# A hybrid mLSTM / Hyena / expert-FFN backbone on one core: the ends of its two expert layers rearranged

## What is computed

```python
def moe_ffn(xt, rg_w, rg_b, re_w, re_b, w13, w2):
    g_prob = softmax(xt @ rg_w + rg_b);  g_w, g_idx = top_k(g_prob, 1)
    e_logits = (xt @ re_w + re_b).reshape(T, 4, 8)[group g_idx]
    e_w, e_idx = top_k(softmax(e_logits), 2);  e_w = e_w / sum(e_w)
    ...                                    # rows sorted by expert
    gate, up = split(xblk @ w13[e], 2);  yb = (silu(gate) * up) @ w2[e]
    return segment_sum(yb * row_w, row_tok)

for i in range(2):
    hl = hl + g1 * mixer_i(norm(hl))
    hl = hl + g2 * moe_ffn(norm(hl), ...)
return rmsnorm(hl, final_g)
```

## Time and profile before

| | us |
|---|---|
| median of 3 runs | 2341.99 (2341.27 to 2342.74) |
| profiled execution, own time | 2345.15 |
| its span in the trace | 2343.4 |
| PE busy in it | 2043.4 (87%) |
| mean DMA rate | 253 GB/s |

### The profile page before, as it was taken

One profiled execution on the slowest core, in us unless ns is written; L12 is line 12 of the kernel. 1 busy time (PEld: TensorE's weight loads), 2 busy tenths in 40 slices (PEclk: granted clock), 3 DMA queues, 4 the chain that ended last, 5 costly groups with the idle time before them and its releaser, 6 DMA issues. The chain is left out here.

```text
span 2343.4 us, 20663 instructions
## 1 busy us (share of the span) xinstructions
PE 2043.4 (87%) x7552; PEld 901.8 (38%) x7552; DVE 819.8 (35%) x1601; ACT 363.7 (16%) x770; POOL 238.5 (10%) x523
## 2 busy tenths in 40 slices
PE   5999899999979969988888859999996998888882
PEld 2555344444433434433223224444554443332320
DVE  2777402256353642211111115463734221111113
ACT  2111202212213121111111103110002111111111
POOL 0000000000000002221112210000000221112220
PEclk9999999999989979999999989999996999999996
DMA  9797612320104569999999963221253999999994
GB/s 348 286 377 293 214 45 90 108 87 22 63 3 143 211 231 372 406 407 407 407 406 406 403 255 128 69 90 36 100 223 117 380 406 407 407 407 406 406 403 155
DMA packets 185926, 593.62 MB, mean 253 GB/s; under 512 B 23880, under 2 KB 41536, under 8 KB 178505
## 3 DMA queue, kind: packets, MB, share of 16 engines
q1 hardware_dynamic: 159230, 549.58, 60.5%
q10 hardware_dynamic: 14412, 25.59, 3.1%
q0 software_dynamic: 12160, 16.83, 2.0%
HBM read 572.68 MB, written 42.31 MB: 262 GB/s over the span
## 5 line engine op out<-in xcount | busy, mean ns | idle before, releaser
L537 PE MATMUL bank<-w,xT 128*64 128x512 f32 x1920 | 436.7, 601 | 55.0 <-DMA w<-in_moe_w 46.8
L557 PE MATMUL bank<-w,hT 128*64 128x512 f32 x1168 | 281.9, 626 | 71.6 <-DMA w<-in_moe_w 64.1
L537 PEld LDWEIGHTS bank<-w,xT 128*64 128x64 f32 x1920 | 151.8, 138 | 327.5 <-issue 270.1
L727 DVE COPY hT<-bank 128x256 f32<-128x256 f32 x73 | 31.0, 424 | 523.4 <-PE bank L545 523.4
L557 PEld LDWEIGHTS bank<-w,hT 128*64 128x64 f32 x1168 | 88.9, 143 | 216.5 <-issue 144.4
L1132 PE MATMUL bank<-uhi,wnh 128*128 128x512 f32 x384 | 168.4, 593 | 0.9 <-ACT uhi L881 0.9
L488 ACT ACTIVATE oh<-bank 128x256 f32<-128x256 f32 x73 | 28.1, 385 | 827.9 <-PE bank L537 827.9
L732 DVE TENSOR_TENSOR ohs<-bank,g2h 128x512 f32<-128x512 f32 x73 | 50.5, 692 | 258.7 <-PE bank L557 258.7
L1511 PE MATMUL bank<-uT,wo 128*128 128x512 f32 x256 | 132.0, 597 | 0.5 <-DVE uT L1399 0.5
L2136 PE MATMUL bank<-ow,yT 128*128 128x512 f32 x256 | 117.1, 612 | 4.5 <-PEq L125 4.5
L1847 PE MATMUL bank<-uT,wo 128*128 128x512 f32 x256 | 110.7, 593 | 0.0
(11 more groups left out here) (425 smaller groups left out, 2124.7 us busy)
## 6 DMA issues: line engine op xcount, KB each, us to landing
w<-in_moe_w SPq DMA_DIRECT2D x177, 2048.0 KB, 24.5
adab<-in_ada_w SPq DMA_DIRECT2D x24, 2048.0 KB, 10.8
w13x<-in_moe_w SPq DMA_DIRECT2D x18, 2048.0 KB, 24.3
wnh<-in_h_in_w SPq DMA_DIRECT2D x12, 1024.0 KB, 5.2
wo<-in_m_in_w SPq DMA_DIRECT2D x4, 2048.0 KB, 10.8
wo<-in_m_in_w ACTq DMA_DIRECT2D x4, 2048.0 KB, 14.4
ow<-in_m_out_w SPq DMA_DIRECT2D x8, 1024.0 KB, 7.1
d_xm<-xmb ACTq DMA_DIRECT2D x16, 385.5 KB, 6.1
```

Source lines behind the costliest of these rows:

```text
L537: ins = t_.matmul(b[n * C:(n + 1) * C, :].rearrange("c (g f) -> c g f", g=2), xT[:, k, half * C:(half + 1) * C], w13s[i][:, k, n], start=( ...
L557: ins = t_.matmul(b_y[m * C:(m + 1) * C, :], hT[:, k, half * C:(half + 1) * C], w2[:, u, kk, m * 512:(m + 1) * 512], start=(kk == 0), stop ...
```

## The change

Four edits:

1. The two semaphores of each expert layer's scatters now belong to the whole program (`s_yst2`). POOL's two last waits on them are gone, and `load_results` has them: SP of the next stage waits. The scatters' source (`ohs`) and index tiles (`six`) are allocated earlier in the stage. POOL's wait in an extra step stays.
2. SP asks for the second layer's router tables in the first layer's routing, once DVE has read the first layer's, no more at the end of the layer.
3. In the last static step PE does `product2` of the block before ahead of `product1` of the last block, DVE scales it ahead of the last block's SwiGLU product, and SP asks for that w2 ahead of the last expert's w13.
4. `hyena` is one stage. Its SP asks for `flo` before `load_results`, and the last stage's SP for `fg` before `load_results`.

```diff
+        s_yst2 = [[sem(f"s_yst{l}{i}") for i in range(2)] for l in range(2)]
...
         def load_results(sp, l, yg, s_yg):
+            for u in range(2):
+                sp.wait_ge(s_yst2[l][u], (NS + u) // 2 * 16)
             for t in range(TL):
                 sp.dma_start(yg[t], ...).then_inc(s_yg[t], 16)
...
-                s_g2 = sem(f"s_g2{l}")
+                s_g2 = sem(f"s_g2{l}"); s_yst = s_yst2[l]
+                ohs = T("ohs", [P, 2 * TL * P]); six = [T(f"six{i}", [P, 1], I32) for i in range(2)]
...
                     def main(s):                                  # SP
                         p = NB + s
+                        if p == NE - 1:
+                            load_second(p - 1, expert(p))
                         if p < NE:
                             load_first(p, expert(1 + p))
-                        if NB < p <= NE:
+                        if NB < p <= NE and p != NE - 1:
                             load_second(p - 1, expert(p))
...
+                    if l == 0:
+                        sp.wait_ge(S["eg1"], 1)
+                        load_route_tables(sp, 1)
                     sp.wait_ge(S["meta"], 1)
                     sp.wait_ge(S["vst"], 16 * TL)
                     steps(sp, main, lambda: None, extra)
...
                         sp.dma_start(dfe[:], ...).then_inc(s_dfe, 16)
-                    if l == 0:
-                        load_route_tables(sp, 1)
...
                     steps(pool, main, drain, extra)
-                    for u in range(2):
-                        pool.wait_ge(s_yst[u], (NS + u) // 2 * 16)
...
                     def main(s):                                  # PE
+                        if s == NS - 1:
+                            h_transposes(s)
+                            product2(s)
                         first(s)
-                        if s > 0:
+                        if 0 < s < NS - 1:
                             h_transposes(s)
                         next_rows(s)
-                        if s > 0:
+                        if 0 < s < NS - 1:
                             product2(s)
...
                     def main(b):                                  # DVE
                         if b > 0:
                             h_turned(b)
+                        if b == NS - 1:
+                            y_out(b)
                         hidden(b)
-                        if b > 0:
+                        if 0 < b < NS - 1:
                             y_out(b)
...
         def hyena():
             with stage() as c:
                 Fs = put("Fs", [P, 2, 4, 3, 512], W13)
                 wn = put("wnh", [P, 2, KD, 256], W2)
-                hyena_mix(Fs, wn, [sem(f"s_wnh{u}") for u in range(2)])
-        def hyena_mix(Fs, wn, s_wn):
-            with stage() as c:
+                s_wn = [sem(f"s_wnh{u}") for u in range(2)]
...
-                    load_results(sp, 0, yg, s_yg)
                     for h in range(2):
                         sp.dma_start(flo[1][:, :, h * 512:(h + 1) * 512], d_fl[2 + h]).then_inc(s_flo, 16)
+                    load_results(sp, 0, yg, s_yg)
...
+                sp.dma_start(fg[:], row_bcast(...)).then_inc(s_fg, 16)
                 load_results(sp, 1, yg, s_yg)
-                sp.dma_start(fg[:], row_bcast(...)).then_inc(s_fg, 16)
```

More of the change, by code:

```diff
@@ L299, in expert_ffn @@
                 i64 = T("i64", [P, 1, P]); ibl = T("ibl", [P, 1, NBLK])
-                ohs = T("ohs", [P, 2 * TL * P]); ohp = ohs[:].rearrange("p (i n) -> p i n", n=P); i65 = T("i65", [P, 1, P]); near = T("near", [P, 2 * TL, 1]); ohb = T("ohb", [P, 2 * TL, NBLK])
+                ohp = ohs[:].rearrange("p (i n) -> p i n", n=P); i65 = T("i65", [P, 1, P]); near = T("near", [P, 2 * TL, 1]); ohb = T("ohb", [P, 2 * TL, NBLK])
                 sli = T("sli", [P, 2 * TL], I32); sbi = T("sbi", [P, 2 * TL], I32); sbf = T("sbf", [P, 2 * TL, 1]); spf = T("spf", [P, 2 * TL, 1])
@@ L310, in expert_ffn @@
                 S = {k: sem(f"s_{k}_l{l}") for k in "vsc vst eg1 eg2 ex1 ex2 sel rk dv tab tps ecs esp iot xz tok gx ea eps gxe meta dst xps xTa xTv upa up sg h hps hT yp ya ix sx".split()}
-                six = [T(f"six{i}", [P, 1], I32) for i in range(2)]
                 shift = modT[:, 3 * l, KD:2 * KD]
@@ L314, in expert_ffn @@
                 yb = [ohs[:, i * (D // 2):(i + 1) * (D // 2)] for i in range(2)]
-                s_yst = [sem(f"s_yst{l}{i}") for i in range(2)]
                 b_gu, b_x, b_h, b_y = (bank[0], bank[1], bank[6]), (bank[2], bank[3]), bank[4], bank[5]
@@ L772, in spectrum, with load_slab @@
             return ins
+        SLABS = [s for part in (2, 0, 1) for s in range(part * 4, part * 4 + 4)]
+        def load_slab(sp, wn, s_wn, q):
+            s = SLABS[q]
+            sp.dma_start(wn[:, q % 2], I["h_in_w"][0].rearrange("(k p) n -> p k n", p=P)[:, :, s * 256:(s + 1) * 256]).then_inc(s_wn[q % 2], 16)
         def hyena():
@@ L777, in hyena @@
                 wn = put("wnh", [P, 2, KD, 256], W2)
-                hyena_mix(Fs, wn, [sem(f"s_wnh{u}") for u in range(2)])
-        SLABS = [s for part in (2, 0, 1) for s in range(part * 4, part * 4 + 4)]
-        def load_slab(sp, wn, s_wn, q):
-            s = SLABS[q]
-            sp.dma_start(wn[:, q % 2], I["h_in_w"][0].rearrange("(k p) n -> p k n", p=P)[:, :, s * 256:(s + 1) * 256]).then_inc(s_wn[q % 2], 16)
-        def hyena_mix(Fs, wn, s_wn):
-            with stage() as c:
+                s_wn = [sem(f"s_wnh{u}") for u in range(2)]
                 def T(name, shape, dt=F32):
@@ L2218, in _ @@
             def _(sp):
+                sp.dma_start(fg[:], row_bcast(I["final_g"].rearrange("(o n) -> o n", o=1))).then_inc(s_fg, 16)
                 load_results(sp, 1, yg, s_yg)
-                sp.dma_start(fg[:], row_bcast(I["final_g"].rearrange("(o n) -> o n", o=1))).then_inc(s_fg, 16)
                 for t in range(TL):
```

## The result

| | before | changed |
|---|---|---|
| median, 20 runs each (us) | 2342.81 | 2347.16 |
| lowest of the runs | 2340.18 | 2343.29 |
| profiled execution, own time | 2345.15 | 2343.58 |
| its span in the trace | 2343.4 | 2341.8 |
| PE busy in it | 2043.4 | 2043.4 |

The ratio is 1.0015, 95% interval 1.0008 to 1.0021: the change costs 3.5 us (1.9 to 4.9), which is within the 0.2% that I had called "the same". The ratio goes by the means; the medians lie 4.35 us apart. One of the 20 runs of before took 2526.03 us and is left out of the ratio. The forecast was +2.4 us and 2344.4 us; 2347.16 lies in the range, near its upper edge. Of the 2.8 us between them 0.8 is the base: before's median is 2342.81 over 20 runs, and the forecast stood on the 2341.99 of three.

What follows compares the result with a forecast made beforehand. Weight streams bound the expert layers; at their ends POOL's drain (first) and PE's jumps (second) come last. Terms 0 + 0 + 1.5 - 0.4 + 1.3 = +2.4 us on the median 2341.99 gave 2344.4 us, range 2336.5 to 2347.5.

Steps and rivals of the forecast that it cites:

- Edit 1, zero: At both expert layers' ends: POOL's last waits for the scatters do not block, so moving them gains 0.
- the waits were the cost: Rival, 10%: without the waits the last stage's loads start 9.6 us earlier and Hyena's PE 3.8 us earlier; 2331.0 us.
- POOL's drain fixed: At the expert layers' ends: POOL's drain, 6.4 and 6.2 us with busy and idle DMA queues, is taken as fixed.
- the drain hangs on the tables: Rival, 10%: the first layer's 6.4 us drain comes from the table loads' small descriptors; Hyena opens 3.8 us earlier, 2340.6 us.
- Edit 2, zero: Router tables: gain 0 at the first layer's end; four loads of 9.5 us fit into 20 us of routing, cost 0.
- The rival that made them delay the stream: Rival, 10%, first layer's routing: table loads wait for queue room, issue ends after 881.73, stream ends 4.8 us late; 2349.2 us.
- Edit 3, +1.5: Second layer's last block: last product 0.9 us later behind its own chain, plus 0.6 us for a scatter inside the stream.
- Edit 4: `fg`, +1.3: Last stage's start: `fg` ahead of the expert rows that DVE waits for costs 1.3 us, between 0.3 and 1.8.
- 512 KB at the stream's rate: Last stage: the step that sizes `fg`'s load, 512 KB ahead of the expert rows taking 1.3 us.
- Edit 4: `flo` first, zero: Hyena's start: `flo`'s 2 MB, 5.1 us, ahead of the expert rows is covered by DVE's and PE's other work; cost 0.
- Edit 4: the stage less, -0.4: Behind Hyena's block: one of two meetings goes, with its clearing, on the path before DVE's routing; -0.4 us.
- The rule: PE's jumps: the skill's 108 ns per compare-and-branch would make the sum 2.2 us lower, +0.2; the trace's durations were used.

Runs made afterwards that it cites:

- e3: The kernel before with the groups of extra blocks nested, so an engine without extra blocks jumps once, not four times: 2340.51 us, ratio 0.9991.
- e4: The changed kernel with the groups of extra blocks nested, so an engine without extra blocks jumps once, not four times: 2343.36 us, ratio 0.9999.
- e7: The changed kernel with one jump, no POOL drain at the expert layers' ends, the old block order and `fg` behind the expert rows: 2328.91 us, ratio 0.9942.
- e10: e7 with the two waits for the last scatters put back at the end of POOL's program: 2328.81 us, ratio 0.9936.
- e1: The changed kernel with `fg` asked for behind the expert rows again: 2342.56 us, ratio 1.0002.
- e6: The changed kernel without POOL's drain at the two expert stages' ends, the meeting behind each clearing by semaphores alone: 2344.8 us, ratio 1.0008.
- e2: The changed kernel with the old order of the last block's products and of the last w2 load: 2345.42 us, ratio 1.0012.
- e5: The changed kernel with the old order of the last block and `fg` behind the expert rows: 2342.26 us, ratio 0.9995.
- e11: e7 with `dfe` asked for ahead of `fle` at the first expert layer's end: 2328.81 us, ratio 0.9938.

## Why the prediction was right, and where not

**Edit 1, zero: right, and for its reason.** The waits had passed, PE and POOL's drain held the meetings. Where POOL is last, with its drain or without, moving the waits is worth 0.25 us (e3 against e4) and 0.03 us (e7 against e10), since POOL's own time behind a scatter is as long as the scatter's landing. The rival "the waits were the cost" falls: its 9.6 us at the last stage are there to be had, 9.4 in e7, but by one jump and no drain, with the waits in either place.

**POOL's drain fixed: right.** It took 6.36 and 6.19 us with the waits and tables gone, as with them. That it would take as long with its scatter still in flight is not shown: in every trace the last scatter had landed when the drain began, 0.1 to 0.5 us before at the second layer's end. The rival "the drain hangs on the tables" falls with that. One aside was wrong: PE's third jump at the first layer stayed at 7.61 us with no table in the queues.

**Edit 2, zero: right.** The loads fit, though they took 15.5 us, not 9.5. The rival that made them delay the stream came within 3.4 us of its condition, nearer than the 10% suggests.

**Edit 3, +1.5: a term too large, 0.9 to 1.1 measured.** The chain was right, 5.98 us against 5.99 read from the extra block, and by itself it gave 0.9. The other part, 0.6 us for a scatter that now falls into the stream, was 0.2 on the landing in the changed kernel and e4 and nothing in e1 and e6 (15.58 and 15.59 us from block 29's `product2`, before 15.60). I had charged the scatter's bytes in full.

**Edit 4: `fg`, +1.3, was mis-sized.** The pairs give 1.9 us (e2 and e5), 2.4 (e4 and e3) and 2.9 (changed and e1) by the traces, all above my upper bound of 1.8; before's own trace against the changed one gives 2.0, because it has the extra wait. The ratios say 3.0 (changed and e1) and 4.0 (e2 and e5), and are too uncertain to size it; those of e4 and e3 differ by 1.9 for the whole change. The step that failed is "512 KB at the stream's rate": behind the rows `fg`'s packets do take the 1.3 us of the DMA engines' time that I had charged (1.27), ahead of them 1.7 to 2.4, and the first packet of the rows moved 1.7 to 2.1 us later; the rest is the rows' own transfer, 0.2 to 0.3 us longer in e2, e4 and e6 and 1.3 in the changed kernel (in before's trace it took as long with `fg` last, 12.0). Why this load, which writes one row to 128 partitions, is slower at the head of a stage was not tried.

**Edit 4: `flo` first, zero: right.** In all 13 traces DVE's first add in Hyena stands right behind its spectra, without a wait for the expert rows. From PE's first spectrum to the transposes it is 43.3 to 43.7 us in the three kernels with `flo` behind the rows and 43.5 to 44.9 in the ten with it ahead, and what differs there is PE's clock: it starts at half in every trace and is granted in full 2.9 to 3.8 us after the first spectrum where the stretch is under 44 us, 4.5 to 6.1 us after it where it is longer.

**Edit 4: the stage less, -0.4: in size not shown.** One meeting, which was 0.4 us in before, has gone; the stretch from Hyena's transposes to the second layer is 345.0 to 345.3 us in the three kernels with both stages and 343.7 to 344.8 in eight with one, 0.2 us and more shorter; the other two are in the last section.

With the measured sizes the sum is 0 + 0 + 1.1 - 0.4 + 2.4 = +3.1 us; the ratio says +3.5 (1.9 to 4.9). That the forecast of +2.4 came so near is in part luck: edit 3 was put 0.4 us too high and `fg` 1.1 us too low.

**The rule.** PE's jumps took 3.0 to 8.4 us in every kernel, not 108 ns, and taking three of them away moved the stage by 3 us until POOL's drain was next (e3). The Trainium skill's figure ("Advanced Engine Details and Errata", Control Flow Timing) does not hold for these branches on PE; on POOL the same ones took 45 ns. For the fetch of the target the trace has this: from 2294 to 2313 of before, around PE's four jumps, the queues for instructions moved 9 packets, 0.12 MB. That PE waited for these is likely, not shown.

## What to carry to other kernels

At a stage's end ask which engine reaches the meeting last and which comes just behind it, before moving any wait: here two costs hid each other and the table loads, and removing one gained 1.6 to 3.7 us by the ratios, which is hardly clear of their noise, both of them 12 to 14. A load that is needed last belongs behind the ones that are waited for, unless other work covers it: 512 KB cost 2 to 3 us in the last stage, and the 2 MB of `flo` nothing in Hyena. An extra block's own chain in the trace gave the price of an order that the main loop does not show to 0.01 us.

## What was unexpected of the hardware

- **A jump on PE costs microseconds.** The branches over absent blocks took 3.0 to 8.4 us on PE, 40 to 50 ns on POOL, ACT and SP. Nested, one of 3.4 to 5.0 us is left at each layer's end.
- **A POOL drain behind indirect DMAs took 6.2 to 6.4 us** in every kernel that had one, though its scatters had landed before it began, and leaving it out put nothing later.
- **A wait for a scatter just issued can be free.** Behind its last scatter POOL came to its next work outside the step 2.4 us after the issue at the earliest, and the data landed 2.3 us after it where POOL had one jump (e3, e4, e7 to e11); put back, the wait passed in 17 ns (e10).
- **PE's clock moved more time than the change.** From the transposes in Hyena to the second layer's start it is 345.0 us in before's trace and 340.5 in that of the changed kernel. Windows of before, then of the changed kernel, near Hyena's end (stretch, us, busy by engine, then the granted clock, here 1.00 for 2.4 GHz and 0.50 for 1.2 GHz, DMA share, GB/s):

```profile
1760.00:1769.00 9.00, 6.73 (x22) 3.18 (x21) 1.99 (x3) 0.66 (x2) 0.00 (x0) 1.00 0.00 0
1770.00:1785.00 15.00, 13.93 (x65) 13.42 (x65) 3.74 (x17) 2.23 (x4) 0.00 (x0) 0.50 0.00 0
```

```profile
1770.00:1774.00 4.00, 4.00 (x39) 4.00 (x37) 0.69 (x1) 1.64 (x3) 0.00 (x0) 1.00 0.00 0
1774.00:1785.00 11.00, 5.71 (x28) 5.20 (x27) 6.02 (x35) 4.04 (x5) 2.71 (x12) 0.51 0.18 55
```

PE fell to half clock at about 1770 in before and at about 1774 in the changed kernel, 4 us more of Hyena's last products at full clock. Of the other traces one (e2) has this short stretch too, 340.3 us, and the rest have 343.7 to 345.3. At Hyena's start PE runs at half clock in both kernels; the changed one began 1.2 us sooner and had 0.1 us of that left at DVE's first add (1410.02, 1410.16), since from 1401 to 1403 its granted clock was 0.71 and that of before 0.94. This is why the changed kernel's profiled span is the shorter one while its median is the longer. Until the fall PE's granted clock had been full for 368.6 us in before and for 372.1 in the changed kernel; e2 has 372.1 too, all the other traces 368.6. What decides it was not tried.
